# Output projection of a decoder layer by one level of Strassen's algorithm, with the combinations made on chip

## The reference

```python
# 1024 prompt tokens and 8*8 = 64 sample tokens, d_model = 1024, float32
xn = _rms(x, g_pre)
proj = xn @ w_in
qa, ka, va, za, qm, km, vm, om, zm, ig, fg = jnp.split(proj, SPLIT_POINTS, axis=-1)
att, wk, wv = attend(qa, ka, va, sinks)          # window 128, 8 heads of 64
a_out = att * jax.nn.silu(za)                    # 512 wide
h, C, n, m = _mlstm(qm, km * (M_HEAD_DIM ** -0.5), vm, i_pre, logf, C0, n0, m0)
h = _rms(h, g_mh)
m_out = jax.nn.sigmoid(om) * h * jax.nn.silu(zm) # 512 wide
y = jnp.concatenate([a_out, m_out], axis=-1) @ w_out
return x + _rms(y, g_post), (wk, wv, C, n, m)
```

## Time and profile before

| | us |
|---|---|
| median of 3 runs | 574.08 (574.03 to 574.48) |
| the profiled execution, its own time | 574.52 |
| its span in the trace | 572.7 |
| TensorE busy in it | 558.8 (98%) |
| VectorE, ScalarE, GpSimd busy | 263.7, 203.9, 134.1 |
| last matmul of the input projection starts | 470.79 |
| last matmul of the output projection starts | 566.68 |

### The profile page before, as it was taken

The page is one execution under the profiler, slowest core; times in us unless marked ns, Lnnn a source line. Parts: engine busy times, 40 slices in busy tenths (PEclk is TensorE's granted clock), DMA queues, the critical chain, the costliest instruction groups (busy, mean ns, idle before and its releaser), DMA issues.

```text
span 572.7 us, 9881 instructions
## 1 busy us (share of the span) xinstructions
PE 558.8 (98%) x4007; PEld 517.1 (90%) x4007; DVE 263.7 (46%) x535; ACT 203.9 (36%) x548; POOL 134.1 (23%) x140
## 2 busy tenths in 40 slices
PE   5999999999999999999999999999999999999996
PEld 5999999999989999999988889899999998888874
DVE  5620011584566556511476868446534437052223
ACT  6852211423544444410546454234332225011011
POOL 1101122122243324412012121236424430011001
PEclk9999999999999999999999999999999999999999
DMA  8852210812111011107023230412112325044231
GB/s 314 290 193 74 67 38 2 276 62 83 38 38 39 1 38 38 39 11 177 2 69 115 75 91 22 112 45 66 39 38 84 100 74 183 1 146 148 100 103 56
DMA packets 32037, 49.93 MB, mean 87 GB/s; under 512 B 4508, under 2 KB 23196, under 8 KB 31976
## 3 DMA queue, kind: packets, MB, share of 16 engines
q1 hardware_dynamic: 31560, 48.77, 26.8%
q10 hardware_dynamic: 432, 0.53, 0.3%
HBM read 41.70 MB, written 8.05 MB: 87 GB/s over the span
## 4 chain that ended last, share of the span: by engine, by line
PE 95%; DVE 2%; issue 1%; DMA 1%; POOL 1%; ACT 0%; DVEq 0%; POOLq 0%; ACTq 0%
PE ps L577 53%; PE ps L515 9%; PE ps L516 8%; PE ps L517 8%; PE ps L626 2%; PE ps L686 2%; PE ps L751 1%; PE ps L727 1%; PE ps L763 1%; PE ps L649 1%; PE ps L520 1%; PE ps L519 1%; PE ps L692 1%; PE ps L753 1%; DMA w_raw<-in_w_in_tiles 1%
## 5 line engine op out<-in xcount | busy, mean ns | idle before, releaser
L577 PE MATMUL ps<-x_hl,w_hi 128*128 128x364 f32 (+1 forms) x1200 | 304.6, 334 | 6.5 <-ACT x_hl L876 6.5
L577 PEld LDWEIGHTS ps<-x_hl,w_hi 128*128 128x128 f32 x1200 | 212.8, 189 | 13.5 <-ACT w_hi L881 6.5
L577 PE MATMUL ps<-x_hl,w_lo 128*128 128x364 f32 (+1 forms) x600 | 198.9, 331 | 0.0
L577 PEld LDWEIGHTS ps<-x_hl,w_lo 128*128 128x128 f32 x600 | 113.7, 189 | 0.1
L1636 POOL TENSOR_TENSOR qmT<-qmT,sg 128x364 f32<-128x364 f32 (+1 forms) x24 | 33.7, 1406 | 51.1 <-DVE sg L1486 30.4
L992 ACT ACTIVATE prob<-prob,nmx 128x192 f32<-128x192 f32 (+1 forms) x64 | 27.9, 437 | 45.8 <-DVE sd L1298 45.8
L515 PE MATMUL ps<-wt_hi,x_hl 128*128 128x324 f32 x128 | 39.9, 312 | 0.0
L517 PE MATMUL ps<-wt_hi,x_hl 128*128 128x324 f32 x128 | 39.8, 311 | 0.0
L516 PE MATMUL ps<-wt_lo,x_hl 128*128 128x324 f32 x128 | 39.8, 311 | 0.0
L1588 POOL TENSOR_TENSOR prob<-prob,rden 128x768 f32<-128x768 f32 (+1 forms) x16 | 22.6, 1414 | 72.2 <-DVE rden L1304 72.2
L334 POOL TENSOR_TENSOR w_lo<-w_raw,w_hi 128x1024 fp32r<-128x1024 f32 x12 | 28.8, 2398 | 42.6 <-ACT w_hi L915 42.6
(11 more groups left out here) (238 smaller groups left out, 889.5 us busy)
## 6 DMA issues: line engine op xcount, KB each, us to landing
w_raw<-in_w_in_tiles SPq DMA_DIRECT2D x24, 512.0 KB, 3.6
x_tok<-in_x_prompt SPq DMA_DIRECT2D x8, 512.0 KB, 4.5
w_raw<-in_w_out_tiles SPq DMA_DIRECT2D x8, 512.0 KB, 3.4
x_res<-in_x_prompt SPq DMA_DIRECT2D x8, 512.0 KB, 4.2
out_y_prompt<-y_out SPq DMA_DIRECT2D x7, 512.0 KB, 2.9
wt_raw<-in_w_tok SPq DMA_DIRECT2D x4, 648.0 KB, 7.2
logw<-lw_rows SPq DMA_DIRECT2D x8, 256.0 KB, 3.9
Cs<-in_state_C SPq DMA_DIRECT2D x16, 128.0 KB, 2.6
```

Source lines behind the costliest of these rows:

```text
L577: last = mm(ps[:, sub_bank(sub), 0:w], wt, xm, start=(at_ == 0), stop=(at_ == 23))
```

## The change

The product is cut into blocks of two. For prompt tiles 2p and 2p+1 (pair p, four pairs) let A11 be the attention half of tile 2p, A21 that of tile 2p+1, A12 and A22 the mLSTM halves; each is 4 feature tiles x 128 tokens. The weight is cut into `a0`, `a1` (attention rows, left and right 512 columns) and `m0`, `m1` (mLSTM rows). One level of the Strassen-Winograd form then needs seven block products of 12 matmuls in place of eight:

- P1 = A11 a0, P2 = A12 m0, P3 = (A12 - S2) m1, P4 = A22 t4, P5 = S1 t1, P6 = S2 t2, P7 = (A11 - A21) t3
- with S1 = A21 + A22, S2 = S1 - A11 of the tokens and t1 = a1 - a0, t3 = m1 - a1, t2 = m1 - t1, t4 = m0 - t2 of the weights.

The sample tile keeps the plain product; its left columns use `a0` and `m0` (16 matmuls), its right ones `a0` + `t1` + `m1` (24 matmuls, since `a1` is no longer split). In all TensorE issues 376 matmuls of 512 columns for the output projection in place of 416.

What each engine gets:

- SyncE loads the weight as four blocks of 1 MB during the gate strips, in place of eight tiles of 512 KB one by one.
- VectorE makes t1, t3 and t2 (`sum_of`) and splits `a0` and t3 during the gate strips, two more token differences and the first two low parts. The splits of `qaT` and `qmT` as a whole are gone; in their place 28 blocks of 4 x 128 x 128 are split one by one (`blk_hi` on ScalarE, `blk_lo` on VectorE).
- GpSimd gets the other two differences for P7, t4, the low part of t1 (`wq_lo`), the three sums of each pair (`sums`), and the residual addition of the first six tiles (`add_res`).
- Bank copies and adds join the partial products: per pair ScalarE copies four banks to SBUF (`s1`, `v7`, `u2`, `c12`) and VectorE adds three banks to SBUF (`c21`, `c22`, `c11`). The norm works on SBUF tiles `ys`, no longer on PSUM.
- TensorE runs all P7, all P1, then P6, P4, P5, P2, P3 of each pair; the sample tile goes ahead of the last pair. A pair owns its two banks; each product waits for its block's low part (`blk_lo`) and for the copy or add that frees its bank.

Core of the diff:

```diff
+        def strassen(name, p, bank, w, lo_name, first, final=True):
+            n = product(name, p)
+            wait(pe, "blk_lo", n + 1)
+            wait_lo(pe, lo_name)
+            for j in range(4):
+                mm(ps[:, bank, :], blk[n][:, 0, j, :], w[:, 0, j, :], start=(first and j == 0), ...)
+                mm(ps[:, bank, :], blk[n][:, 0, j, :], w[:, 1, j, :], start=False, ...)
+                last = mm(ps[:, bank, :], blk[n][:, 1, j, :], w[:, 0, j, :], start=False, ...)
+            last.then_inc(s("prod"), 1)
...
-        for p in range(4):
-            out_part(p, list(range(4, KT)))
...
+            strassen("P7", p, 2 * p + 1, wq["t3"], "t3", True)
+        for p in range(NPAIR):
+            strassen("P1", p, 2 * p, wq["a0"], "a0", True)
+        for p in range(NPAIR):
+            if p == NPAIR - 1:
+                sample_half(0)
+                sample_half(1)
+            wait(pe, "s1_done", p + 1)
+            strassen("P6", p, 2 * p, wq["t2"], "t2", False)
+            wait(pe, "v7_done", p + 1)
+            strassen("P4", p, 2 * p + 1, wq["t4"], "t4", False)
+            wait(pe, "u2_done", p + 1)
+            strassen("P5", p, 2 * p, wq["t1"], "t1", False)
+            wait(pe, "c21_done", p + 1)
+            strassen("P2", p, 2 * p + 1, wq["m0"], "m0", True)
+            wait(pe, "c22_done", p + 1)
+            strassen("P3", p, 2 * p, wq["m1"], "m1", False)
...
+        def blk_lo(n):
+            wait(dve, "blk_hi", n + 1)
+            TT(blk[n][:, 1], block_source(n), blk[n][:, 0].bitcast(F32), ALU.subtract).then_inc(s("blk_lo"), 1)
...
+        def sums(p):
...
+                wait(pool, "prod", r + 5)
...
+            b2, b1, b4 = (raw_blk[N_FIRST + r + c][:] for c in (0, 2, 4))
+            step(add(b1, qaT[:, :, half(p, 1)], qmT[:, :, half(p, 1)], ALU.add))
+            step(add(b2, b1, qaT[:, :, half(p, 0)], ALU.subtract))
+            add(b4, qmT[:, :, half(p, 0)], b2, ALU.subtract).then_inc(s("sums"), 1)
...
+        def add_res(e):
...
+            Q.tensor_tensor(y, y, x_res[0:n, e % 2, :], ALU.add).then_inc(s("y_pool"), 1)
...
+        for p in range(NPAIR):
+            if p < NPAIR - 1:
+                sums(p + 1)
+                rs(2 * p)
+                add_res(2 * p)
+                rs(2 * p + 1)
+                add_res(2 * p + 1)
```

More of the change, by code:

```diff
@@ new lines, in sample_half @@
+        def sample_half(q):
+            wait(pe, "os_ready", 1)
+            wait(pe, "c12_done", 1)
+            wait(pe, "c11_done", 1)
+            parts = [(0, "a0")] + ([(0, "t1"), (4, "m1")] if q else [(4, "m0")])
+            for c, (k0, name) in enumerate(parts):
+                wait_lo(pe, name)
+                for j in range(4):
+                    last = split_products(ps[:, q, :], o_hl_s[:, k0 + j], o_hl_s[:, k0 + j], wq[name][:, 0, j, :], wq[name][:, 1, j, :],
+                                          first=(c == 0 and j == 0), final=(c == len(parts) - 1 and j == 3))
+            last.then_inc(s("ys_done"), 1)
@@ new lines, in _ @@
+        for n in range(3, 7):
+            blk_lo(n)
+        dve_wq_lo("m1")
+        blk_lo(7)
+        dve_wq_lo("t4")
+        wait(dve, "os_hi", 1)
+        for q, src_ in enumerate((qaT, qmT)):
+            last = TT(o_hl_s[:, 4 * q:4 * q + 4, 1, :], src_[:, :, T_P:T], o_hl_s[:, 4 * q:4 * q + 4, 0, :].bitcast(F32), ALU.subtract)
+        last.then_inc(s("os_ready"), 1)
+        blk_lo(N_FIRST)
+        blk_lo(N_FIRST + 1)
+        dve_wq_lo("m0")
+        for n in range(N_FIRST + 2, N_FIRST + 5):
+            blk_lo(n)
@@ new lines, in _ @@
+        wait(pool, "sub_done", NSUB)
+        wait(pool, "ag_done", G)
+        for p in (2, 3):
+            add(raw_blk[p][:], qaT[:, :, half(p, 0)], qaT[:, :, half(p, 1)], ALU.subtract).then_inc(s("s3_sum_pool"), 1)
+        pool.wait_ge(s("wo_ld"), 64)
+        wait(pool, "wo_sum", halves_of(SUM_ORDER, "t2"))
+        for h in range(2):
+            c = slice(2 * h, 2 * h + 2)
+            add(raw_t4[:][:, c], w_out_raw["m0"][:, c], w_out_raw["a1"][:, c], ALU.subtract).then_inc(s("t4_sum"), 1)
@@ L1649, in build @@
+        for h in range(2):
+            wait(pool, "wo_hi", halves_of(HI_ORDER, "t1", h + 1))
+            wq_lo(Q, "t1", h)
+        pool.wait_ge(s("t1_lo"), 2)
+        sums(0)
+        for p in range(NPAIR):
+            if p < NPAIR - 1:
+                sums(p + 1)
[3 more added lines that the diff above has]
+                add_res(2 * p + 1)
+            else:
+                for e in (6, 7, 8):
+                    rs(e)
     block.__exit__(None, None, None)
```

460 lines of the change are left out of this document (293 added, 167 removed).

## The result

| | before | after |
|---|---|---|
| median of 4 runs each, us | 574.08 (574.03 to 574.48) | 578.12 (576.92 to 578.87) |
| span of the profiled execution | 572.7 | 577.1 |
| first matmul of the output projection | 470.96 | 470.38 |
| last matmul of the output projection | 566.68 | 570.16 |
| the stage (last start + 0.23 - first start) | 95.95 | 100.01 |

After / before is 1.0064, with a 95% interval of 1.0051 to 1.0076: the changed kernel is 0.64% slower, though it issues 40 matmuls fewer. The predicted time was 577.1. The profiled execution is the one of 578.87, the slowest of the four, so the losses read from its trace lie at the upper end.

The account below looks back on a forecast made before the run. TensorE was taken as the bound, 95% of the span. Terms -9.4 + 0.7 + 6.8 + 0.3 + 2.2 + 2.2 + 0.4 = +3.2, rounded to +3.0 on 574.1, gave 577.1 us; range 571.5 to 580.0.

Parts of the forecast that it names:

- TensorE's list: Output projection: 376 matmuls for 416, at distances of 0.2269 to 0.2342, take 86.5 us, 9.4 less.
- Third P7: Start of the output projection: VectorE's low part of blk2 waits for GpSimd's second token difference; 0.7 us late.
- Fourth P7: Early output projection: blk3's low part comes late as GpSimd and VectorE alternate on t4, t2 and t1; 6.8 us late.
- the turns: GpSimd and VectorE exclude each other on two-input SBUF work and alternate; a waiter gets in about 0.14 before the other's end.
- P6 of pair 0: First pair: blk8's copy and low part let it start at 500.5, TensorE is there at 500.2; 0.3 us late.
- P6 of pair 2: Third pair: norms, residuals, sums and copies chain to 15.7 us against TensorE's 13.8; 2.2 us late, bounds 1 and 3.5.
- The clock: Behind the 6.8 us gap TensorE runs at 1.2 GHz for up to 6 us; 2.5 us lost, bounds 0 and 3.
- The tail: Kernel end: the last tile's residual load lands later than VectorE's last step needs it; 0.4 us, bounds 0 and 1.
- The gate strips: Before the output projection: weight-block loads and VectorE's added work are hidden by the strips; no cost.
- the harmless turns: Rival: VectorE gets in ahead of GpSimd or both run side by side; 567.5 us, milder form 572.7; together 0.18.
- the held clock: Rival: the gap is as computed but the clock falls too late or recovers at once; 574.8 us, chance 0.20.
- saturation: Rival: exclusive GpSimd and VectorE work per pair outgrows TensorE's time, pairs 1 and 3 wait too; 581 us, chance 0.10.

Follow-up runs that it names:

- best version: Changed kernel with GpSimd's first-phase work and residual additions on VectorE and region E's four block slots moved up 160 bytes: 565.18 us, ratio 0.9836.
- the run of the first phase on VectorE: Changed kernel with token differences, t4, t1's low part and pair 0's sums moved from GpSimd to VectorE, blk3 to blk5 ahead of t2: 570.03 us, ratio 0.9923.
- the run of the order alone: Changed kernel with only blk3 to blk5 split ahead of weight t2 instead of behind it, on VectorE and ScalarE: 576.90 us, ratio 1.0046.

## Why the prediction was right

The time came out at 578.12 for a predicted 577.1, slower with a likelihood of 0.62, and inside the range. The mechanism held as well, VectorE held up by GpSimd and the clock low behind the gap; some of the closeness is luck, which is counted at the end of this section. By its steps:

- *TensorE's list.* Predicted 86.5, and 86.6 is left when gaps and low clock are taken off. The distances were right for each region, the reason given for them was not: it is the place within 256 bytes, not 64, and the 32 bytes account for some 0.0017 of 0.0075.
- *Third P7, 0.7 late.* 0.59.
- *Fourth P7, 6.8 late.* 6.60. It was to start 15.6 behind the projection's end and started 15.5 behind. Each link (t4, t2, t1's first half, blk3) is in the rows; the price per column that was carried over from 360 columns to 512 held (1.29), and the turns were shown by themselves in the kernel before.
- *P6 of pair 0, 0.3 late.* No gap, since the low clock ahead of it had already used more than 0.3, as the sum had counted it.
- *P6 of pair 2, 2.2 late.* 2.08, with GpSimd's residuals ahead of its sums as the sum had it. GpSimd stands idle twice in this chain, 4.00 and 1.40 for VectorE's norms, so it is a chain of dependent steps and not a lack of capacity. The changed kernel's rows, GpSimd and then ScalarE:

```profile
517.47 2.84 POOL L1861 TENSOR_TENSOR y<-y,x_res 128x1024 f32<-128x1024 f32 x1 [4.00 <-DVE y L1679]
...
522.63 2.41 POOL L1861 TENSOR_TENSOR y<-y,x_res 128x1024 f32<-128x1024 f32 x1 [1.40 <-DVE y L1679]
525.00 1.29 POOL L1829 TENSOR_TENSOR raw_blk<-qaT,qmT 128x512 f32<-128x512 f32 x1
...
531.23 0.57 ACT L1200 ACTIVATE y<-ps 128x512 f32<-128x512 f32 x1
```

- *The clock, 2.5.* 2.51 behind the long gap. What the sum missed is a **second fall behind the gap of 2 us**, 1.64 more. The prediction weighed the clock at the long gap alone and gave the short one no price. Whether it comes in every run is open. In the four runs of the changed kernel the mean granted clock is 0.988 at 578.87 and 578.73, 0.992 and 0.991 at 576.92 and 577.50, and a stretch of 3.4 us at half clock is 0.003 of the span. But with the residuals back on VectorE, where the second gap is gone, it ranges from 0.988 to 0.993 as well: a first low stretch of varying length can give the same spread.
- *The tail, 0.4.* 0.9. The wait for `x_res` is there (0.49, below), and it alone sets the start of VectorE's last step: 2.90 behind the last matmul's start, where it was 2.11 before (568.79 - 566.68). That is 0.8, and the last store's landing took 0.1 more. VectorE's last norm products and GpSimd's small addition to the mean square take turns too, and that addition of one column is listed at 0.59, but this costs nothing here: in the best version it is listed at 0.19, and the last step starts 2.95 behind the last matmul's start all the same (559.44 - 556.49), released by the same load.

```profile
571.29 0.68 DVE L1721 TENSOR_TENSOR y<-y,g_post_b 128x512 f32<-128x512 f32 x1
...
571.43 0.59 POOL L1853 TENSOR_TENSOR stat<-stat,stat 128x1 f32<-128x1 f32 x1 [1.27 <-ACT junk L1267]
...
573.06 1.42 DVE L1726 SCALAR_TENSOR_TENSOR y<-y,stat,x_res 128x512 f32<-128x512 f32 x2 [0.49 <-DMA x_res<-in_x_prompt]
```

and of the best version:

```profile
557.75 0.19 POOL L1870 TENSOR_TENSOR stat<-stat,stat 128x1 f32<-128x1 f32 x1 [1.10 <-ACT junk L1266]
...
559.44 1.42 DVE L1743 SCALAR_TENSOR_TENSOR y<-y,stat,x_res 128x512 f32<-128x512 f32 x2 [0.36 <-DMA x_res<-in_x_prompt]
```

- *The gate strips, nothing.* The output projection started at 470.38, not later than before (470.96).

Together: +4.1 for the stage where the terms made +2.8, +0.9 for the tail where they made +0.4, and an input projection that ended 0.58 sooner in this execution, which is +4.4 in span; the medians differ by 4.0. So the terms, +3.2 in all, were 1.8 short of the +5.0 that they stand for in this trace. Two things that nobody predicted brought the result closer: the input projection's earlier end, which differs by some tenths between the traces of all runs (470.4 to 471.0), and a median below the profiled execution. That is luck. The term that was mis-sized is the clock (4.15 for 2.5). Of the rivals, the harmless turns are refuted by the rows, the held clock by the granted clock, and saturation by pairs 1 and 3, which had no gap. That last rival was badly posed: its own sum, 14.7 us of exclusive work against 13.8, was over the limit without the 15% that it asked for, and no wait came of it.

## What to carry to other kernels

Before work is spread over VectorE and GpSimd, count the operations of both that read only SBUF as one queue (two-input operations, and VectorE copies like the one of 1.33 above): if VectorE has such work at the same time, an operation that takes GpSimd 2.40 and VectorE 1.22 is cheaper on VectorE even when GpSimd is idle. Here, with VectorE busy for little more than half of the span, moving them back turned +0.6% into -1.5%. A stage with fewer matmuls is only faster if its operands are ready, so price each gap twice, once as a wait and once as clock that may be lost behind it, the gaps of 2 us too. If two matmuls of one shape stand at different distances, look at where their stationary operands lie before anything else.

## What the runs showed of the hardware that I had not expected

- The start address of the stationary operand sets the distance of fp32r matmuls of 128 x 128 by 512. At 128 bytes above a multiple of 256 they stand 0.2267 apart, at 0 above 0.2325, at 224 above 0.2342. It was seen in two kernels, with `a_hl` moved one way, `m_hl` the other and four block slots; other places, other widths and the reason are open. A shift of 160 bytes took 1.5 us from the kernel before.
- The size of a gap alone doesn't tell whether the clock falls. Behind 2.08 us (from 529.55) it fell to 0.50 at once, in the run of the first phase on VectorE behind 2.05 us it fell 1.4 us late, and in the run of the order alone it stayed at 1.00 behind 2.2 us and again behind 2.08 us ahead of P6 of pair 2, the very gap behind which it fell in the changed kernel. Nor does the gap set the length of the low stretch: behind 6.6 us it was 5.2 us in one trace and 3.85 in another. The Trainium skill (TensorE: Matmul & The Clock Gate, "HAM oscillation — how this bites in real kernels") tells only of longer gaps than these of 2 us. What else decides was not isolated.

The stretches behind the gap of 2.2 us in the run of the order alone, which ends at 490.30, and behind its gap of 2.08 us, which ends at 531.44 (columns as above):

```profile
491.00:494.00 3.00, 3.00 (x15) 2.28 (x14) 3.00 (x4) 0.00 (x0) 1.32 (x1) 1.00 0.00 0
...
532.00:535.50 3.50, 3.50 (x16) 2.82 (x15) 2.27 (x3) 2.52 (x5) 1.75 (x1) 1.00 0.00 0
```

- A GpSimd operation of one column pays for a turn like a long one: 0.59 for 0.19.
- A VectorE copy with one input in SBUF takes turns with GpSimd as well: 1.33 for 0.43, in the run of the kernel before with GpSimd kept busy.
